# Splitting each weight unit on GpSimd in four quarters instead of one instruction per half

## The reference

```python
def layer(x, p, l, mod, ctx):
    g = p['norm_w'][l]
    def half_ffn(x, j, s):
        h = modulate(rmsnorm(x, g[2 * s]), mod[:, 3 * s], mod[:, 3 * s + 1])
        y = swiglu(h, p['ffn_w1'][l, j], p['ffn_w3'][l, j], p['ffn_w2'][l, j])
        return x + 0.5 * mod[:, 3 * s + 2][:, None] * rmsnorm(y, g[2 * s + 1])
    x = half_ffn(x, 0, 0)
    h = modulate(rmsnorm(x, g[2]), mod[:, 3], mod[:, 4])
    y, new = token_mixing(h, p, l, ctx)   # h @ w_in, four groups of heads, concat @ w_out
    x = x + mod[:, 5][:, None] * rmsnorm(y, g[3])
    x = half_ffn(x, 1, 2)
    return x, new
```

## Time and profile before

| | us |
|---|---|
| median of 3 runs | 3450.99 |
| lowest, highest | 3434.47, 3455.9 |
| the profiled execution | 3443.74 |
| its span | 3442.0 |

### The profile page before, as it was taken

The page is one execution under the profiler, slowest core; times in us unless marked ns, Lnnn a source line. Parts: engine busy times, 40 slices in busy tenths (PEclk is TensorE's granted clock), DMA queues, the critical chain, the costliest instruction groups (busy, mean ns, idle before and its releaser), DMA issues.

```text
span 3442.0 us, 49578 instructions
## 1 busy us (share of the span) xinstructions
PE 3089.8 (90%) x21080; PEld 2914.7 (85%) x21080; DVE 1176.2 (34%) x1613; ACT 526.2 (15%) x866; POOL 1143.6 (33%) x388
## 2 busy tenths in 40 slices
PE   6999998978888889999779999989789888999996
PEld 3999898868877889999749999989688777899996
DVE  3110112363565454133331101133635654531332
ACT  2000001211112321001120000121112132210111
POOL 1344335313021324444314444443131113344442
PEclk9999999979788989999869999999797889999998
DMA  6332332101011111221163333321010101122211
GB/s 248 139 118 91 129 128 87 46 35 41 28 43 50 37 49 66 75 86 58 34 225 122 119 105 124 119 78 51 30 53 16 65 28 49 40 71 79 74 66 56
DMA packets 45630, 271.92 MB, mean 79 GB/s; under 512 B 5120, under 2 KB 10752, under 8 KB 19520
## 3 DMA queue, kind: packets, MB, share of 16 engines
q1 hardware_dynamic: 38736, 259.99, 21.1%
q10 hardware_dynamic: 6768, 10.11, 0.9%
HBM read 265.35 MB, written 4.73 MB: 78 GB/s over the span
## 4 chain that ended last, share of the span: by engine, by line
PE 41%; DVE 5%; ACT 2%; issue 1%; DMA 1%; DVEq 1%; ACTq 0%; PEldq 0%; SPq 0%
PE ps L460 12%; PE ps L462 12%; PE ps L461 12%; PE ps L654 1%; DMA first_raw<-in_w_mod 1%; ACT arena L854 1%; ACT rstd L854 1%; PE ps L622 1%; PE ps L661 1%; PE ps L471 1%; DVE rstd L1205 1%; PE ps L613 0%; PE ps L639 0%; DVE rstd L1160 0%; PE ps L492 0%
## 5 line engine op out<-in xcount | busy, mean ns | idle before, releaser
L460 PE MATMUL ps<-h,wsplit 128*128 128x320 f32 (+1 forms) x3520 | 1104.0, 314 | 57.2 <-DVE rstd L1205 25.6
L461 PE MATMUL ps<-h,wsplit 128*128 128x320 f32 (+1 forms) x3520 | 1093.5, 311 | 0.0
L462 PE MATMUL ps<-h,wsplit 128*128 128x320 f32 (+1 forms) x3520 | 1093.4, 311 | 0.0
L419 POOL TENSOR_SCALAR wsplit<-raw 128x2048 fp32r<-128x2048 f32 (+1 forms) x192 | 333.3, 1736 | 2239.7 <-issue 1032.4
L421 POOL TENSOR_TENSOR wsplit<-raw,wsplit 128x2048 fp32r<-128x2048 f32 (+1 forms) x192 | 810.1, 4219 | 16.0
L460 PEld LDWEIGHTS ps<-h,wsplit 128*128 128x128 f32 (+1 forms) x3520 | 663.9, 189 | 83.5 <-DVE rstd L1205 45.7
L461 PEld LDWEIGHTS ps<-h,wsplit 128*128 128x128 f32 (+1 forms) x3520 | 664.0, 189 | 0.5
L462 PEld LDWEIGHTS ps<-h,wsplit 128*128 128x128 f32 (+1 forms) x3520 | 663.2, 188 | 0.5
L460 PE MATMUL ps<-hidden,wsplit 128*128 128x320 f32 x1408 | 436.1, 310 | 7.7 <-DVE hidden L1208 4.8
L462 PE MATMUL ps<-hidden,wsplit 128*128 128x320 f32 x1408 | 435.1, 309 | 0.0
L461 PE MATMUL ps<-hidden,wsplit 128*128 128x320 f32 x1408 | 435.0, 309 | 0.0
(11 more groups left out here) (173 smaller groups left out, 2759.5 us busy)
## 6 DMA issues: line engine op xcount, KB each, us to landing
raw<-in_w SPq DMA_DIRECT2D x88, 1024.0 KB, 6.2
raw<-in_w_mod SPq DMA_DIRECT2D x48, 1024.0 KB, 4.8
raw<-in_w SPq DMA_DIRECT2D x64, 704.0 KB, 4.1
raw<-in_w_in SPq DMA_DIRECT2D x30, 1024.0 KB, 4.8
first_raw<-in_w_mod SPq DMA_DIRECT2D x24, 1024.0 KB, 4.9
raw<-in_w_out SPq DMA_DIRECT2D x8, 1024.0 KB, 5.0
arena<-in_rpb ACTq DMA_DIRECT2D x2, 1792.0 KB, 7.2
xT<-in_x ACTq DMA_DIRECT2D x1, 2560.0 KB, 11.2
```

The lines of the kernel that those rows point to most:

```text
L419: nc.gpsimd.tensor_scalar(w[:, 0], src, 1.0, 1.0, ALU.mult, ALU.mult).then_inc(pool_hi, 1)
L460: mm(out, w[0], x[0], start=first, stop=False)
L461: mm(out, w[0], x[1], start=False, stop=False)
L462: return mm(out, w[1], x[0], start=False, stop=last)
```

## The change: four quarters

Each `split` runs four `tensor_scalar` on quarters of the columns (512 of 2048, 352 of 1408, 320 of 1280), then four `tensor_tensor` on the same quarters. Each of the latter waits for the `tensor_scalar` of its own quarter. `pool_hi` and `split_done` count four for a unit where they counted one; the PE and SP wait for the fourth.

```diff
+PARTS = 4
@@
-        SD = lambda n: SPLIT.index(n) + 1
+        SD = lambda n: PARTS * (SPLIT.index(n) + 1)
@@ load, SP
-                            sp.wait_ge(split_done, i * ds + SD(n - SLOTS))
+                            sp.wait_ge(split_done, i * (ds * PARTS) + SD(n - SLOTS))
@@ split, POOL
-                        nc.gpsimd.tensor_scalar(w[:, 0], src, 1.0, 1.0, ALU.mult, ALU.mult).then_inc(pool_hi, 1)
-                        pool.wait_ge(pool_hi, i * 2 + (k + 1))
-                        nc.gpsimd.tensor_tensor(w[:, 1], src, w[:, 0].bitcast(FP), ALU.subtract)\
-                            .then_inc(split_done, 1)
+                        step = words // PARTS
+                        for q in range(PARTS):
+                            at = slice(q * step, (q + 1) * step)
+                            nc.gpsimd.tensor_scalar(w[:, 0, at], src[:, at], 1.0, 1.0, ALU.mult, ALU.mult)\
+                                .then_inc(pool_hi, 1)
+                        for q in range(PARTS):
+                            at = slice(q * step, (q + 1) * step)
+                            pool.wait_ge(pool_hi, i * (2 * PARTS) + (k * PARTS + q + 1))
+                            nc.gpsimd.tensor_tensor(w[:, 1, at], src[:, at], w[:, 0, at].bitcast(FP), ALU.subtract)\
+                                .then_inc(split_done, 1)
@@ claim, PE
-                        pe.wait_ge(split_done, i * 2 + SD(n))
+                        pe.wait_ge(split_done, i * (2 * PARTS) + SD(n))
```

## The result

| | before | quarters |
|---|---|---|
| median, us | 3444.95 | 3399.78 |
| lowest, highest | 3434.47, 3455.9 | 3392.69, 3402.29 |
| span of the profiled execution | 3442.0 | 3397.6 |
| mean granted clock of the PE | 0.924 | 0.929 |

The times of before are those of the table ahead with one run more. The ratio is 0.9865, with a 95% interval of 0.9827 to 0.9903. Lines behind the edit have moved by 7: L1208 is now L1215, L1160 is L1167, L497 is L504, L622 is L629, L1637 is L1644.

A forecast was written before the change was run, and what follows sets the result against it. The PE, busy 90%, was taken as the bound, with POOL mattering only where somebody waits for it. Per layer 3.9 + 3.9 + 2.7 + 1.4 - 0.5 - 1 = 10.4, two layers 21: 3451 - 21 = 3430 us, range 3408 to 3468.

The forecast's parts named there:

- Turns at each quarter: Main case: DVE gets in at POOL's quarter boundaries, waiting 0.6 or 1.35 us instead of up to 4.5; chance 0.60.
- DVE kept out: Rival: back-to-back quarters make DVE wait for all eight POOL instructions; 16 us slower, 3467 us; chance 0.23.
- The price of a split: POOL's eight instructions for a weight unit take 7.9 us, 1.3 us more than now.
- the claims: First feed-forward: PE needs two or three units a layer before POOL's later split is done; 1 us a layer lost.
- Both norms: End of first feed-forward and after `w_out`: DVE's eighth addition of squares ends sooner, 3.9 us gained at each.
- D: Token-mixing stage: DVE's L1571, L1577 and L1579 are held up less, so the PE goes on 2.7 us sooner a layer.
- L1208: this step: 84 DVE subtractions lose up to 4 us each now, about 1.3 then; nobody waits for them, gain nothing.
- Gates of C: DVE's dense run of gate instructions and scans in stage C lets quarters by; 0.5 us lost a layer.
- the sign that L1477 keeps its place within 2 us: Stage C: the end of DVE's gate run, L1477, should stay within 2 us of its place if the forecast holds.
- scans do not wait: Rival: DVE scans in stage C run beside POOL unhindered; 10 us a layer more gained, 3409 us; chance 0.10.
- B: First softmax: DVE's scaling gets in at an earlier POOL boundary, ending the PE's wait 1.4 us sooner a layer.
- The sum: All terms together: 10.4 us a layer, 21 us in two layers, giving a median of 3430 us.

The follow-up runs named there:

- halves: The changed kernel with each split in two parts instead of four: 3423.59 us, ratio 0.9928 to the kernel before.
- eighths: The changed kernel with each split in eight parts instead of four: 3410.02 us, ratio 0.9907 to the kernel before.
- the second profile: The changed kernel run and profiled once more with no edit: 3401.66 us, ratio 0.9866 to the kernel before.
- the transposes: The changed kernel plus 64 identity transposes on the PE ahead of its wait for the gates in stage C: 3404.58 us, ratio 0.9851 to the kernel before.

## Why the prediction was wrong, step by step

**Turns at each quarter: right.** A waiting DVE instruction is served at the boundary. L1208 takes 1280 ns (under 1600 forecast), addition 8 takes 0.87 us, the wait of L497 is 3.9 us (about 4 forecast). The Trainium skill, SBUF — State Buffer, section "SBUF: two separate sides", says that whoever starts first holds the shared ports for the whole instruction and that the other fully blocks. The trace agrees at the scale of one quarter: each L1208 that meets POOL ends 0.68 or 0.69 us after the quarter in progress. The rival "DVE kept out", which rested on overlapping memsets and on the Trainium skill, GPSIMD Engine Reference, section Instruction dispatch, falls: DVE's L1578 and L1584 run between eight queued quarters, and no L1208 waits for more than the part in progress.

**The price of a split: too high, without effect.** A split that DVE does not hold up takes 7.4 us, 0.8 more than before, within the bounds of 0.2 and 2.1 us. I took 1.3. Starts lie 0.58 and 1.25 us apart; with halves it is 1.01 and 2.37, with eighths 0.37 and 0.70. That is 0.84 and 2.2 ns a word and a fixed part of 0.15 and 0.14 us, where I took 0.2 and 0.35. My working had a slip besides: with 4.63 us and 2.0 ns a word the fixed part comes to 0.5 us, not 0.15. The tightest unit of the earlier trace rows keeps 0.25 us:

```profile
340.21 5.04 POOL L428 TENSOR_TENSOR wsplit<-raw,wsplit 128x512 fp32r<-128x512 f32 x4
...
345.50 0.41 PE L467 MATMUL ps<-h,wsplit 128*128 128x320 f32 x1 [0.67 <-DVE rstd L1212]
```

So the claims cost 0 and not 1 us a layer. (Even with 1.3 us my rows gave two late units in layer 1 and one in layer 2, 0.4 us a layer.) The eighths show what lies beyond.

**Both norms: right.** 3.9 us each were forecast; 3.65 to 3.75 and once 3.59 came. The wait itself fell by 4.01 us. Some is given back behind it, where DVE's next pair of two-operand instructions (L1200; L1193 before) meets POOL's later end: 2.96 us instead of 1.56.

**D: this step failed.** "2.7 us" was the stall of DVE, and it measured 2.96. What failed is that the term ended there, "the PE goes on at 974.20 after 3.90 us of idling". What the PE does next was in the trace of before, just behind the row of L622 in the earlier trace rows, which shows the first 4 of 12:

```profile
974.20 2.96 PE L622 MATMUL ps<-arena 128*128 128x128 f32 x12 [3.90 <-DVE arena L1330]
```

These 12 instructions took 2.96 us where they take 1.94 after, and the granted clock was 0.58 over 22 us. I never read the granted clock. The price of the slow stretch was 7.7 us a layer, 2.6 times the idle time saved. The Trainium skill, TensorE: Matmul & The Clock Gate, section "Why this matters for your kernels", advises against long idle gaps of the PE between bursts of matmuls. The profiles agree: behind waits of 3.40 to 4.03 us at this place there was half clock each time, for 23.9 us in all or more in ten layers of twelve and for 6.8 in two; behind 0.94 to 1.22 us none or one stretch of 3.4 us, except with eighths (17.1 and 20.5 us behind 1.02), which that advice does not cover.

**L1208: this step failed too.** "Nobody waits for them within the unit of 14 us: nothing." True for ten of eleven in a group. For the eleventh a row of the waits view said otherwise (4.8 us in 4 waits), and the step went by the unit's length instead of by that row. The four that matter are not even among the 84; they write another type and have a row of their own in the view of the earlier trace rows:

```profile
L1208 DVE TENSOR_TENSOR hidden<-rstd,hidden 128x640 fp32r<-128x640 f32 x4 | 12.3, 3084 | 3.2 <-ACT hidden L854 3.2
```

Price: 5.8 us. That all 84 lose up to 4 us was wrong as well: 44 of them lose nothing.

**Gates of C: wrong sign, small.** 0.5 us lost was forecast; DVE's run is 2.6 us shorter, so the sign that L1477 keeps its place within 2 us failed too. I let every instruction of the run meet a quarter, but POOL's split ends at 699.66 in the changed kernel, and the next nine instructions run free. The rival "scans do not wait" falls as well: they wait.

**B: right in place, given back.** The wait fell by 1.67 us (1.4 forecast), and at a lower granted clock behind it 2.2 were lost again in layer 1.

**The sum.** The stalls that I listed measured 3.7 + 3.65 + 3.0 + 1.7 + 2.6 = 14.6 us a layer, where the sum had 10.4. Of C's and B's 4.3 us nothing reached the end in the second profile; the stages behind lost it again, B's at a lower granted clock. That leaves 10.3 us, 21 in all, as forecast. This match is luck: the norms brought 0.4 less and D's stall 0.3 more, B's 1.4 did not arrive, and the 0.5 of C and the 1 of the claims were not lost. The other half of the gain, 15.4 us of clock in D and 5.8 in the down units, stood in no term.

## What to carry to other kernels

A stall of the PE costs more than its length when the granted clock falls behind it. Read the granted clock of the stretch behind each wait before pricing it: where what follows is PE work, the gain from shortening the wait enough is the wait plus what the same work costs more at half clock (7.1 us in 22 here). It is not the rule everywhere: half clock follows the shortened wait of 3.9 us at the norms too, and C did not gain from the transposes. Where POOL and DVE both work in SBUF, the longest POOL instruction is what a DVE instruction on the path can lose; cut it where such an instruction stands (two splits of 96 in each layer for the norms and two for D bring 35 of the 41 us here), and not below the point where the split itself gets late.

## What the runs showed of the hardware

- A full clock can be kept by work that is of no use: 24 repeated matmul instructions of 0.12 us made a stage 7.1 us shorter; 48 of them, longer than the wait, made it no shorter.
- The clock's stretches at 1.2 GHz differ between executions and between the two identical layers. The start of C's next unit moved by 6.5 us between two profiles of the same program, and D with whole splits by -5.6 to +7.2; so a single profile says little on a stage with such stretches. The steps at norms, D with quarters and down units came again to 0.3 us and say much.
- The DVE subtraction L1208 (128x640, two SBUF operands), where it meets POOL, ends 0.67 to 0.70 us after the POOL instruction in progress, whatever that one's length: 220 of 220 in five kernels.
- Eight POOL instructions in a row, also without a wait between them, do not keep DVE out. POOL's `tensor_scalar` quarters start 0.06 us sooner than the recorded end of the one before them: 512 columns last 0.64 us by record and follow one another at 0.58.
- Halves gave the norms as much as quarters, and D nothing: a lone instruction loses what is left of one part, a run of three loses up to three.
